# Two up projections with seven block products in place of eight in 19 of 22 tile pairs

## The chip, the core and the metric

One core of one Trainium2 chip runs the whole program. The time is the device time in microseconds. The kernel before took 1276.48 us, the median of three runs (1274.92 to 1276.8).

## The reference, cut to what matters

The model has two layers over 528 tokens (16 meta tokens and 512), width 1024, float32. Layer 0 mixes by a state-space model, layer 1 by differential attention; each is followed by this channel mixer, with D_FF = 2816:

```python
def conv_ffn(h, w_up, conv_w, conv_b, w_down):
    L = h.shape[1]
    up = h @ w_up                                   # (528, 1024) @ (1024, 5632)
    up_p = jnp.pad(up, ((0, 0), (CONV_WIDTH - 1, 0), (0, 0)))
    c = conv_b + sum(conv_w[j] * up_p[:, j:j + L] for j in range(CONV_WIDTH))
    gate, val = jnp.split(c, 2, axis=-1)
    return (jax.nn.silu(gate) * val) @ w_down       # (528, 2816) @ (2816, 1024)
```

In front of it h is normalized by rms_norm: each token by one over the root of its mean square plus 1e-6, and each channel by a gain.

## The kernel before

Everything is kept with channels on the 128 partitions and tokens along the free dimension. Float32 accuracy is had by splitting: each operand is a high part, rounded to the format that TensorE multiplies (ACT does it, `split_hi`, L297), and a low part, the rest (POOL, `split_lo`, L301). A product is three matmuls: high by high, high by low, low by high.

A unit is a weight tile of 1024 x 128, loaded by one DMA of 512 KB into one of two slots of `raw`. Its split parts go into `wH` and `wL`, four slots each. `unit_products` (L314) multiplies it by the eight tiles of the activation, for two halves of the tokens (264 columns each in layer 0, 258 in layer 1): 48 matmuls into two PSUM banks. An up projection is 22 pairs of units, a gate tile and a value tile, so 96 matmuls a pair; two pairs share the eight banks in turn.

Rounded activations are `hgH` and `hgL`, with the gain in them but not the root, which is per token and is multiplied in when DVE drains the banks into `u` (L1796, L1797). For the root, POOL sums squares into `acc` while the mixer's last projection is written (L2027, L2028), four matmuls with ones add them up (`stat_products`, L854), ACT takes the root (L1391) and DVE the reciprocal `rstd` (L1787). In the first pair the statistics stand behind 108 matmuls of the projection: both units of pair 0, and two of the eight tiles of the next unit.

Per pair DVE does, all in SBUF: two drains, the last conv tap with the bias for gate and value (TENSOR_SCALAR, L1801), two more taps of each (L1807), the product of silu and value (L1814) and the low part of the result (L1816). ACT does two weight roundings, the silu (L1402) and the rounding of the result into `actH` (L1404). POOL does two weight low parts. The order on each engine is the order of the code, in loops of two pairs; semaphores such as `up_free` (banks drained), `w_lo` (low part there), `w_used` (slot free) join the engines.

The down projection follows. In layer 0 it is 8 groups of 22 tiles by 6 matmuls of 264 columns. In layer 1 (`down_by_token`, L937) the activation is the stationary side: per tile 24 matmuls of 512 columns into all eight banks, which first take the residual by transposes (L927).

## Time and profile before

| | us |
|---|---|
| median of the runs | 1276.48 |
| span of the profiled execution | 1273.0 |
| TensorE busy (matmul) | 1243.4 |
| DVE busy | 751.6 |
| POOL busy | 607.4 |
| ACT busy | 570.7 |

The runs list no time of the profiled execution by itself. The median of the runs is 3.5 us above its span; that difference is taken for what lies around the span. Busy times of different engines overlap. A group of instructions is told by its line; L297, L301 and L314 are helpers called from several stages.

### The profile page before, as it was taken

To read this page: it belongs to the slowest core of one execution; us is meant where nothing else is said; L and a number is where in the kernel's file an instruction comes from. 1 tells how busy PE (TensorE), PEld (TensorE's weight loads), DVE (VectorE), ACT (ScalarE), POOL (GpSimd) and SP (SyncE) were. 2 spreads that over 40 slices of the span, in tenths; PEclk is the share of its full clock that TensorE was granted. 3 is DMA by queue.
4 is the path that set the end of the run, shared out by engine and by line. 5 is a ranking of instruction groups with operands and counts; after the bars stand their busy time and mean duration, and the time that the engine had idled before them with its cause. 6 is when DMAs were issued, how large, how long until landed. Compare 5 with 4: busy or idle time off the path is not lost.

```text
span 1273.0 us, 26292 instructions
## 1 busy us (share of the span) xinstructions
PE 1243.4 (98%) x10335; PEld 1185.3 (93%) x10335; DVE 751.6 (59%) x1028; ACT 570.7 (45%) x957; POOL 607.4 (48%) x361
## 2 busy tenths in 40 slices
PE   5899999999999999999999999999999999999998
PEld 5888999999999999999998988989999999998886
DVE  8997122688888884111455555553688888882002
ACT  7996543343343432222656656633243333432113
POOL 5433566444444345656654544419544344444431
PEclk9999999999999999999999999999999999999999
DMA  8333332223322333333222112113323333233231
GB/s 174 67 72 82 102 100 84 75 75 99 99 82 87 95 95 91 93 91 112 70 69 65 50 51 68 34 50 100 97 71 97 99 96 86 82 99 99 99 99 66
DMA packets 179498, 108.88 MB, mean 86 GB/s; under 512 B 7100, under 2 KB 173789, under 8 KB 179165
## 3 DMA queue, kind: packets, MB, share of 16 engines
q1 hardware_dynamic: 178997, 107.31, 30.0%
q8 instruction: 51, 0.84, 0.3%
q10 hardware_dynamic: 432, 0.59, 0.1%
q14 instruction: 18, 0.15, 0.0%
HBM read 101.59 MB, written 2.10 MB: 81 GB/s over the span
## 4 chain that ended last, share of the span: by engine, by line
PE 86%; issue 6%; POOL 4%; DVE 2%; ACT 1%; DMA 0%; SPq 0%; POOLq 0%; DVEq 0%; ACTq 0%
PE ps L314 49%; PE ps L987 10%; PE ps L937 10%; PE ps L818 7%; PE ps L1024 2%; PE ps L1094 2%; PE ps L772 1%; POOL acc L2028 1%; PE ps L764 1%; PE ps L1070 1%; POOL sqt L2027 1%; PE ps L1028 0%; PE ps L744 0%; DVE ps L1727 0%; PE ps L711 0%
## 5 line engine op out<-in xcount | busy, mean ns | idle before, releaser
L301 POOL TENSOR_TENSOR wL<-raw,wH 128x1024 fp32r<-128x1024 f32 x182 | 446.9, 2467 | 548.8 <-ACT wH L297 523.0
L314 PE MATMUL ps<-hgH,wH 128*128 128x264 f32 (+1 forms) x1408 | 285.3, 284 | 0.0
L314 PE MATMUL ps<-hgH,wL 128*128 128x264 f32 (+1 forms) x1408 | 285.3, 284 | 0.0
L314 PE MATMUL ps<-hgL,wH 128*128 128x264 f32 (+1 forms) x1408 | 285.0, 284 | 0.0
L297 ACT ACTIVATE wH<-raw 128x1024 fp32r<-128x1024 f32 x182 | 186.4, 1048 | 216.4 <-PE ps L314 79.0
L314 PEld LDWEIGHTS ps<-hgH,wH 128*128 128x128 f32 x1408 | 218.9, 189 | 0.1
L314 PEld LDWEIGHTS ps<-hgL,wH 128*128 128x128 f32 x1408 | 218.4, 189 | 0.0
L314 PEld LDWEIGHTS ps<-hgH,wL 128*128 128x128 f32 x1408 | 217.8, 189 | 0.0
L1402 ACT ACTIVATE cg<-cg 128x528 f32<-128x528 f32 (+1 forms) x44 | 28.2, 640 | 266.7 <-DVE cg L1807 266.7
L1807 DVE SCALAR_TENSOR_TENSOR cg<-u,PV,cg 128x528 f32<-128x528 f32 (+1 forms) x88 | 104.9, 1192 | 13.0 <-DVE cv L1801 6.7
L1801 DVE TENSOR_SCALAR cv<-u,PV 128x528 f32<-128x528 f32 (+1 forms) x44 | 111.3, 2530 | 0.0
L987 PE MATMUL ps<-hgH,wH 128*128 128x264 f32 x384 | 83.2, 298 | 0.0
L987 PE MATMUL ps<-hgH,wL 128*128 128x264 f32 x384 | 78.2, 285 | 0.0
L987 PE MATMUL ps<-hgL,wH 128*128 128x264 f32 x384 | 77.9, 284 | 0.0
L314 PE MATMUL ps<-actH,wL 128*128 128x264 f32 x352 | 71.2, 283 | 0.0
L314 PE MATMUL ps<-actH,wH 128*128 128x264 f32 x352 | 71.2, 283 | 0.0
L314 PE MATMUL ps<-actL,wH 128*128 128x264 f32 x352 | 71.2, 283 | 0.0
L1807 DVE SCALAR_TENSOR_TENSOR cv<-u,PV,cv 128x528 f32<-128x528 f32 (+1 forms) x88 | 66.2, 752 | 0.0
L1829 DVE TENSOR_TENSOR ytok<-ps,fgain 128x512 f32<-128x512 f32 x4 | 2.8, 692 | 103.2 <-ACT ysq L1421 103.2
L1465 ACT ACTIVATE Pb<-ps,tiny 128x144 f32<-128x144 f32 (+4 forms) x66 | 34.8, 532 | 63.2 <-DVE tiny L1855 63.1
L987 PEld LDWEIGHTS ps<-hgH,wH 128*128 128x128 f32 x384 | 59.3, 189 | 3.9 <-issue 3.8
L1763 DVE SCALAR_TENSOR_TENSOR hgL<-hT,PV,hgH (+1 forms) x24 | 34.9, 1455 | 43.2 <-ACT hgH L1373 43.2
(301 smaller groups left out, 2384.8 us busy)
## 6 DMA issues: line engine op xcount, KB each, us to landing
raw<-ffn_w_up SPq DMA_DIRECT2D x88, 512.0 KB, 3.8
raw<-ffn_w_down SPq DMA_DIRECT2D x38, 512.0 KB, 3.6
raw<-attn_w_qkv SPq DMA_DIRECT2D x24, 512.0 KB, 3.7
raw<-s_w_glu SPq DMA_DIRECT2D x16, 512.0 KB, 4.0
TT<-KD SPq DMA_DIRECT2D x64, 64.0 KB, 2.4
raw<-attn_w_o SPq DMA_DIRECT2D x8, 512.0 KB, 4.1
raw<-ffn_w_down SPq DMA_DIRECT2D x8, 384.0 KB, 3.4
xb<-x SPq DMA_DIRECT2D x8, 256.0 KB
```

The lines of the kernel that those rows point to most:

```text
L297: nc.scalar.activation(wH[:, slot, 0:nk], raw[:, slot % 2, 0:nk], ACT.Copy).then_inc(w_hi, 1)
L301: nc.gpsimd.tensor_tensor(wL[:, slot, 0:nk], raw[:, slot % 2, 0:nk], wH[:, slot, 0:nk].bitcast(F32), ALU.subtract).then_inc(w_lo, 1)
L314: mm = nc.tensor.matmul(ps[:, bank + b, 0:tw], w[:, slot, k0 + k, :], x[:, kt, t0:t0 + tw], start=first and k == 0 and s0, stop=last and k ...
L818: mm = nc.tensor.matmul(ps[:, bank + b, 0:tw], w[:, n % 4, k, :], x[:, k, t0:t0 + tw], start=k == 0 and s0, stop=k == 7 and s1)
L937: mm = nc.tensor.matmul(ps[:, 2 * t + c, :], x[:, kt, tok], w[:, n % 4, 4 * c:4 * c + 4], start=False, stop=last and w is ws[-1] and x is ...
L987: mm = nc.tensor.matmul(ps[:, unit_bank(n) + b, 0:tw], w[:, n % 4, k, :], x[:, k, t0:t0 + tw], start=k == 0 and s0, stop=k == 7 and s1)
L1024: return nc.tensor.matmul(ps_row[:, base[c] + a:base[c] + b], q[half[c], q0:nk], k[half[c], a:b], start=True, stop=stop)
L1402: nc.scalar.activation(cg[:, t0:], cg[:, t0:], ACT.Silu).then_inc(silu_set[l], 1)
L1465: ins = nc.scalar.activation(Pb[:, c, 0:nk], score_row(i, c), ACT.Exp, bias=mn[:, c:c + 1], scale=-1.0, accum_out=esum[:, c:c + 1])
L1763: V.scalar_tensor_tensor(hgL[:, ds(ct, 1)], hT[:, ds(ct, 1)], PV[:, ds(gain, 1)], hgH[:, ds(ct, 1)].bitcast(F32), ALU.mult, ALU.subtract). ...
L1801: ins = V.tensor_scalar(c[k][:, t0:], u[:, k, 2 + t0:2 + L], col(i, CONV_W + (3 * l + 2) * 2 * FT + k * FT + q), col(i, CONV_B + l * 2 * F ...
L1807: ins = V.scalar_tensor_tensor(c[k][:, t0:], u[:, k, t0 + j:L + j], col(i, CONV_W + (3 * l + j) * 2 * FT + k * FT + q), c[k][:, t0:], ALU. ...
```

## The change

The first three pairs of each layer stay as they are ("plain"). For each of the other 19 ("fast"), numbered s = 0 to 18, the pair is a 2 x 2 block product: the weights in two halves of the inner dimension (four tiles each) by gate and value, the activation in the same two halves by two halves of the tokens. Eight block products become seven of the Winograd form of Strassen's method, P1 to P7, each 4 tiles x 3 = 12 matmuls of one token half's width into one bank.

- Weight side: AA is the gate tile itself (both halves), A22 the value tile's second half, S1, S2, S3 and S4 are sums and differences of halves. DVE forms the four sums, S1 in PSUM bank 3 and the others in `Wsum`. ACT rounds all of them; POOL takes the low parts of AA, S2 with S3, S4 and A22, DVE that of S1.
- Activation side: seven factors (four quarters and T1 to T4), once per layer, from the normalized activation: `normed` makes the quarters with the gain and `rstd`, `factors` the four differences; ACT rounds seven; POOL takes the low parts of four, DVE of three. They lie where `actH` and `actL` were.
- Result side: P1, P6, P5 and P3 accumulate into one bank of the pair, P7 and P4 into the next, P2 into bank 2. ACT copies the bank after P1, P6 and P5 (`snap`), and as the last quarter (`top_right`); DVE adds three quarters into `u` or `u2`.
- The order on TensorE is P1(s), P2(s), P3(s-1), P6(s), P7(s), P4(s-1), P5(s).
- The conv of a fast pair runs in banks 6 and 7: ACT writes the last tap with the bias there, DVE adds the two others in place, gate first, then value. The last tap of plain pairs moves from DVE to ACT too.
- `act32` holds the product of silu and value; its 22 high and low parts are made after the last step's products free the factors' place.
- In the first pair the statistics stand behind 66 matmuls.
- Loops are written out. In layer 1 the token tiles use other banks, and the load of the final gain is issued on SP's queue.

TensorE, the start and the fast pairs:

```diff
+PLAIN = 3
+FAST = FT - PLAIN
...
+                    for c, k0, nk in ((0, 0, CT - 1), (1, 0, CT // 2), (1, CT // 2, CT // 2 - 1), (0, CT - 1, 1), (1, CT - 1, 1)):
+                        if l == 0 and c and k0 == 0:
+                            pe.wait_ge(glu_sig, CT)
+                        if k0 == CT // 2:
+                            stat_products(2 * l)
...
+                def product(name, s, weights, part, f, bank, first):
+                    if weights != "S1":
+                        pe.wait_ge(f_lo_pool, 4 * FAST * l + LOW_POOL[weights, s] + 1)
+                    else:
+                        pe.wait_ge(f_lo_dve, FAST * l + LOW_DVE[weights, s] + 1)
+                    at = ring(l, weights, s).start + part
+                    xH, xL = FB[:, high_at(f), :, 0:width], FB[:, low_at(f), :, 0:width]
+                    for k in range(4):
+                        for i, (w, x) in enumerate(((wHB, xH), (wHB, xL), (wLB, xH))):
+                            mm = nc.tensor.matmul(ps[:, bank, 0:width], w[:, at, k, :], x[:, k], start=first and k == 0 and i == 0,
+                                                  stop=k == 3 and i == 2, skip_group_check=True)
...
+                def free_banks(s):
+                    if s < 2:
+                        pe.wait_ge(up_free[l], PLAIN + s + FREE)
+                    else:
+                        pe.wait_ge(c12_set, FAST * l + s - 1)
+                        pe.wait_ge(c21_set, FAST * l + s - 1)
+                    return chain_bank(s), chain_bank(s) + 1
...
+                def fast(s):
+                    y, z = free_banks(s)
+                    if s == 0:
+                        pe.wait_ge(fb_hi, 7 * l + F_B11 + 1)
+                        pe.wait_ge(fb_lo_pool, 4 * l + 1)
+                    product("P1", s, "AA", 0, F_B11, y, True)
+                    if s == 0:
+                        pe.wait_ge(fb_hi, 7 * l + F_B21 + 1)
+                        pe.wait_ge(fb_lo_pool, 4 * l + 2)
+                    if s:
+                        pe.wait_ge(c11_set, FAST * l + s)
+                    product("P2", s, "AA", 1, F_B21, W_BANK, True)
+                    if s:
+                        third(s - 1)
+                    pe.wait_ge(snap1, FAST * l + s + 1)
+                    if s == 0:
+                        pe.wait_ge(fb_lo_dve, 3 * l + 1)
+                    product("P6", s, "S23", 0, F_T2, y, False)
+                    if s == 0:
+                        pe.wait_ge(fb_lo_dve, 3 * l + 2)
+                    product("P7", s, "S23", 1, F_T3, z, True)
+                    if s:
+                        fourth(s - 1)
+                    pe.wait_ge(snap2, FAST * l + s + 1)
+                    if s == 0:
+                        pe.wait_ge(fb_lo_dve, 3 * l + 3)
+                    product("P5", s, "S1", 0, F_T1, y, False)
```

TensorE, the end of the up stage and the first group of layer 0's down projection, and the start of layer 1's:

```diff
+                    else:
+                        down_part(g, 0, 0, 6)
+                        third(FAST - 1)
+                        fourth(FAST - 1)
+                        down_part(g, 0, 6, 8)
+                    down_part(g, 1, 0, 8)
+                    down_part(g, 2, 0, 6)
...
+                ready(0)
+                products(0, 2, range(2))
+                pe.wait_ge(c11_set, FAST + FAST)
                 residual(3)
+                products(0, 3, range(2))
+                last_products()
+                ready(1)
+                for t in (2, 3):
+                    products(1, t, range(2))
+                pe.wait_ge(c12_set, FAST + FAST)
+                pe.wait_ge(c21_set, FAST + FAST)
+                residual(0)
+                pe.wait_ge(act_set, FT + FT)
+                residual(1)
                 for kt in range(FT - 4):
-                    ready(kt)
```

ACT, the order of the start and of a step:

```diff
+                direct_top(0)
+                plain_taps(0)
+                sums_23(0)
+                factor_high(F_B11, 4)
+                factor_high(F_B21, 8)
+                factor_high(F_T2, 11)
+                factor_high(F_T3, 10)
+                factor_high(F_T1, 9)
+                factor_high(F_B22, 8)
+                factor_high(F_T4, 12)
+                plain_taps(1)
+                for s in range(FAST):
+                    more = s + 1 < FAST
+                    sum_1(s)
+                    if s >= 2:
+                        silu(s - 2)
+                    direct_last(s)
+                    if s >= 2:
+                        val_in(s - 2)
+                    first_snap(s)
+                    if s == 0:
+                        plain_silu(0)
+                    if more:
+                        direct_top(s + 1)
+                    else:
+                        tile_high(0)
+                    if s:
+                        top_right(s - 1)
+                    if not more:
+                        tile_high(1)
+                        down_high(0, "P2")
+                    second_snap(s)
+                    sum_4(s)
+                    if s < 2:
+                        plain_silu(s + 1)
+                    if s:
+                        gate_in(s - 1)
+                    else:
+                        plain_taps(2)
+                    if more:
+                        sums_23(s + 1)
+                    else:
+                        tile_high(2)
+                        down_high(1, "P7")
+                        tile_high(3)
+                    third_snap(s)
+                silu(FAST - 2)
+                for kt in range(4, 6):
+                    tile_high(kt)
+                val_in(FAST - 2)
+                for kt in range(6, 10):
+                    tile_high(kt)
+                top_right(FAST - 1)
+                gate_in(FAST - 1)
+                for kt in range(10, 12):
+                    tile_high(kt)
+                silu(FAST - 1)
+                down_high(2, "P3")
+                val_in(FAST - 1)
+                for kt in range(12, 16):
+                    tile_high(kt)
```

DVE, the order of the start, of a step and of the end, with three of the operations:

```diff
+                def normed(ct):
+                    h = span(hT[:, ct], spans)
+                    gain = GAIN_FFN + 8 * l + ct
+                    second = FBf[:, 0, ct, 0:width] if ct < 4 else FBf[:, low_at(F_B22), ct - 4, 0:width]
+                    first = FBf[:, low_at(F_B11 if ct < 4 else F_B21), ct % 4, 0:width]
+                    scales = span(rstd, spans)
+                    V.scalar_tensor_tensor(first, h[:, 0], PV[:, gain:gain + 1], scales[:, 0], ALU.mult, ALU.mult)
+                    V.scalar_tensor_tensor(second, h[:, 1], PV[:, gain:gain + 1], scales[:, 1], ALU.mult,
+                                           ALU.mult).then_inc(fb_set, 1)
...
+                def bottom_left(s):
+                    dve.wait_ge(f_used, len(PROD) * l + PROD["P4", s] + 1)
+                    V.tensor_tensor(quarter(PLAIN + s, 1, 0, spans), snap[:, 1 + s % 2, 0:width],
+                                    ps[:, chain_bank(s) + 1, 0:width], ALU.add).then_inc(c21_set, 1)
...
+                def bank_tap(s, c, j):
+                    o = conv_bank(l)
+                    return V.scalar_tensor_tensor(o, span(u_pair(PLAIN + s)[:, c, j:L + j], CONV_SPANS[l]), weight(PLAIN + s, c, j), o,
+                                                  ALU.mult, ALU.add)
...
+                drain(0)
+                first_sums()
+                for ct in range(CT):
+                    normed(ct)
+                factors()
+                drain(1)
+                factor_low(F_T2)
+                factor_low(F_T3)
+                factor_low(F_T1)
+                n = plain_taps(0, 1)
+                sum_4(0)
+                after(n)
+                n = plain_taps(0, 0)
+                weight_low("S1", 0)
+                after(n)
+                multiply(0)
+                drain(2)
+                for s in range(FAST):
+                    more = s + 1 < FAST
+                    if s:
+                        bottom_right(s - 1)
+                    if s:
+                        weight_low("S1", s)
+                    if more:
+                        sum_1(s + 1)
+                    if s < 2:
+                        n = plain_taps(s + 1, 1)
+                        after(n)
+                        last = plain_taps(s + 1, 0)
+                    else:
+                        last = val_tap_0(s - 2, val_tap_1(s - 2))
+                    if more:
+                        sum_2(s + 1)
+                    else:
+                        tile_low(0)
+                    if s < 2:
+                        after(last)
+                        if s == 0:
+                            top_left(0)
+                        else:
+                            multiply(2)
+                    else:
+                        bank_multiply(s - 2, last)
+                    if more:
+                        sum_3(s + 1)
+                        sum_4(s + 1)
+                    else:
+                        tile_low(1)
+                    if s:
+                        n = gate_tap_1(s - 1)
+                        bottom_left(s - 1)
+                        gate_tap_0(s - 1, n)
+                    if not more:
+                        tile_low(2)
+                    if s:
+                        top_left(s)
+                    else:
+                        multiply(1)
+                bottom_right(FAST - 1)
+                tile_low(3)
+                tile_low(4)
+                n = val_tap_1(FAST - 2)
+                tile_low(5)
+                n = val_tap_0(FAST - 2, n)
+                tile_low(6)
+                bank_multiply(FAST - 2, n)
+                for kt in range(7, 10):
+                    tile_low(kt)
+                n = gate_tap_1(FAST - 1)
+                bottom_left(FAST - 1)
+                gate_tap_0(FAST - 1, n)
+                for kt in range(10, 12):
+                    tile_low(kt)
+                n = val_tap_1(FAST - 1)
+                tile_low(12)
+                n = val_tap_0(FAST - 1, n)
+                tile_low(13)
+                bank_multiply(FAST - 1, n)
+                for kt in range(14, FT):
+                    tile_low(kt)
```

POOL:

```diff
+                weight_low("AA", 0)
+                weight_low("S23", 0)
+                factor_low(F_B11, 9)
+                factor_low(F_B21, 12)
+                factor_low(F_B22, 11)
+                weight_low("A22", 0)
+                weight_low("AA", 1)
+                weight_low("S4", 0)
+                factor_low(F_T4, 12)
+                weight_low("S23", 1)
+                weight_low("A22", 1)
+                for s in range(2, FAST):
+                    weight_low("AA", s)
+                    weight_low("S4", s - 1)
+                    weight_low("S23", s)
+                    weight_low("A22", s)
+                weight_low("S4", FAST - 1)
+                for j in range(4):
+                    split_lo(pool, nd + j, (nd + j) % 4, 8 if l else (8, 8, 6, 8)[j])
```

## Rows read from the trace of the kernel before

**Rows 1.** The page: engines, granted clock and the chain by engine.

```profile
PE 1243.4 (98%) x10335; PEld 1185.3 (93%) x10335; DVE 751.6 (59%) x1028; ACT 570.7 (45%) x957; POOL 607.4 (48%) x361
...
PEclk9999999999999999999999999999999999999999
...
PE 86%; issue 6%; POOL 4%; DVE 2%; ACT 1%; DMA 0%; SPq 0%; POOLq 0%; DVEq 0%; ACTq 0%
```

**Rows 2.** Window of layer 0's up stage: length, then busy time (instructions) of each engine.

```profile
232.00:485.00 253.00, 253.00 (x2069) 252.90 (x2068) 218.50 (x217) 99.06 (x109) 111.88 (x45) 1.00 0.30 89
```

**Rows 3.** The chain that ended last, in order: start, length, what.

```profile
218.63 13.17 PE ps L314 x108
...
232.69 373.09 PE ps L314 x3060
...
900.63 240.77 PE ps L314 x2004
```

**Rows 4.** Timeline of DVE and POOL: start, length, engine, line, operation, [idle before].

```profile
401.74 2.67 DVE L1807 SCALAR_TENSOR_TENSOR cg<-u,PV,cg 128x528 f32<-128x528 f32 x1 [0.15 <-DVE cv L1801]
...
681.03 2.38 POOL L301 TENSOR_TENSOR wL<-raw,wH 128x1024 fp32r<-128x1024 f32 x1 [3.51 <-ACT wH L297]
...
682.36 1.21 DVE L1866 SCALAR_TENSOR_TENSOR Ab<-Pb,tiny 128x144 f32<-128x144 f32 x1
...
857.20 2.35 DVE L1763 SCALAR_TENSOR_TENSOR hgL<-hT,PV,hgH 128x528 fp32r<-128x528 f32 x1 [1.01 <-ACT hgH L1373]
...
858.93 1.54 POOL L2027 TENSOR_TENSOR sqt<-hT 128x528 f32 x1
...
248.48 1.42 DVE L1801 TENSOR_SCALAR cg<-u,PV 128x528 f32<-128x528 f32 x1 [0.19 <-DVE u L1797]
...
249.82 2.63 DVE L1801 TENSOR_SCALAR cv<-u,PV 128x528 f32<-128x528 f32 x1
```

**Rows 5.** Groups by line and shape: busy, mean ns | idle before.

```profile
L297 ACT ACTIVATE wH<-raw 128x1024 fp32r<-128x1024 f32 x176 | 181.5, 1055 | 192.7 <-PE ps L937 73.2 <-PE ps L314 55.2 <-PE ps L818 23.9
...
L1807 DVE SCALAR_TENSOR_TENSOR cv<-u,PV,cv 128x528 f32<-128x528 f32 x44 | 33.5, 761 | 0.0
...
L1796 DVE TENSOR_TENSOR u<-ps,rstd 128x528 f32<-128x528 f32 x22 | 15.4, 702 | 0.2 <-PE ps L314 0.2
...
L1663 DVE TENSOR_TENSOR E<-E,tmpE 128x1024 f32<-128x1024 f32 x8 | 9.7, 1218 | 0.2
...
L551 POOL TENSOR_TENSOR F2b<-P,Bsw 128x512 f32<-128x512 f32 x8 | 9.2, 1174 | 4.3 <-PE ps L744 4.3
...
L1946 DVE TENSOR_TENSOR hT<-hT,ps 128x258 f32<-128x258 f32 x16 | 6.0, 411 | 3.1 <-PE ps L1136 3.1
```

**Rows 6.** Timeline of POOL and DVE at the start of layer 0's up stage.

```profile
224.10 1.77 POOL L2028 TENSOR_TENSOR acc<-acc,sqt 128x528 f32<-128x528 f32 x1
...
233.46 3.45 DVE L1787 RECIPROCAL rstd<-sqt 128x528 f32<-128x528 f32 x1 [8.76 <-ACT sqt L1391]
...
241.54 0.77 DVE L1807 SCALAR_TENSOR_TENSOR cg<-u,PV,cg 128x528 f32<-128x528 f32 x1 [0.15 <-DVE cv L1801]
...
242.22 0.76 DVE L1807 SCALAR_TENSOR_TENSOR cv<-u,PV,cv 128x528 f32<-128x528 f32 x1
```

**Rows 7.** Timeline of TensorE and DVE at the start of layer 1's up stage.

```profile
885.51 0.40 PE L314 MATMUL ps<-hgH,wH 128*128 128x258 f32 x2
...
899.47 1.16 PE L854 MATMUL ps<-acc,ones 128*128 128x264 f32 x4 [0.83 <-POOL acc L2028]
...
901.40 3.45 DVE L1787 RECIPROCAL rstd<-sqt 128x528 f32<-128x528 f32 x1 [8.12 <-ACT sqt L1391]
```

**Rows 8.** TensorE after an idle stretch: timeline row, then window with PEclk.

```profile
37.04 0.47 PE L709 MATMUL ps<-cst,F1b 128*128 128x128 f32 x1 [2.82 <-POOL F2b L551]
...
38.00:40.00 2.00, 2.00 (x11) 2.00 (x11) 1.93 (x4) 1.98 (x8) 2.00 (x3) 0.50 0.61 105
```

More of the change, by code:

```diff
@@ new lines, in ffn, with down_by_token @@
+                for g in range(CT):
+                    if g:
+                        pe.wait_ge(h_new[1], g - 1 + FREE)
+                        down_part(g, 0, 0, 8)
+                    else:
[5 more added lines that the diff above has]
+                    down_part(g, 2, 0, 6)
+            def down_by_token(last_products):
@@ new lines, in silu, with tile_high @@
+                def silu(s):
+                    act.wait_ge(conv_gate, FT * l + PLAIN + s + 1)
+                    nc.scalar.activation(span(conv_pair(PLAIN + s)[0], CONV_SPANS[l]), conv_bank(l), ACT.Silu).then_inc(silu_set, 1)
+                def tile_high(kt):
+                    act.wait_ge(act_set, FT * l + kt + 1)
+                    for before, t in (("P1", 0), ("P2", 4), ("P6", 8), ("P7", 12), ("P5", 16), ("P3", 20)):
+                        if kt == t:
+                            act.wait_ge(f_used, len(PROD) * l + PROD[before, FAST - 1] + 1)
+                    nc.scalar.activation(act32H[:, kt, t0:], act32[:, act_tile(kt), t0:], ACT.Copy).then_inc(act_hi, 1)
@@ L1406, in ffn @@
+                down_high(3, "P4")
+                for kt in range(16, FT):
+                    tile_high(kt)
                 if l == 0:
@@ L1783, in ffn, with step, drain @@
                 nu, nd = (U_UP0, U_DN0) if l == 0 else (U_UP1, U_DN1)
+                width = spans[0][1]
+                weight = lambda p, c, j: PV[:, CONV_W + (3 * l + j) * 2 * FT + c * FT + p:][:, 0:1]
+                steps = [0]
+                def step(ins):
+                    ins.then_inc(conv_step, 1)
+                    steps[0] += 1
+                    return steps[0]
+                def drain(p):
+                    dve.wait_ge(w_used, nu + 2 * p + 2)
+                    bank = 4 * (1 - p % 2)
+                    for c in range(2):
+                        ins = V.tensor_tensor(span(u_pair(p)[:, c, 2:2 + L], spans), pspan(bank // 2 + c, spans),
+                                              span(rstd, spans), ALU.mult)
+                    ins.then_inc(up_free[l], 1)
```

575 lines of the change are left out of this document (440 added, 135 removed).

## The prediction

> **What bounds the kernel now.** I read the page first. TensorE is busy 98% of a 1273.0 us span at the full granted clock, DVE 59%, ACT 45%, POOL 48%; the chain that ended last runs 86% over TensorE [rows 1]. So only TensorE time counts, unless another engine makes it wait. A window over layer 0's up stage says the same: TensorE idles nowhere in 253 us, and DVE, busy 218.5 us, is the next engine [rows 2]. The chain in order of time gives the pace: 3060 matmuls of 264 columns in 373.09 us, 0.1219 us each, and 2004 of 258 columns in 240.77 us, 0.1201 us each [rows 3].
>
> The last view to read is how DVE and POOL meet. A POOL subtraction with two SBUF inputs ran from 681.03 to 683.41; a DVE operation of 144 elements with two SBUF inputs, started at 682.36, took 1.21 us and ended 0.16 us behind POOL. At 401.74 such an operation took 2.67 us [rows 4] where its like takes 0.77 [rows 6]. The other way round, POOL's square, started at 858.93 under a DVE operation that ended at 859.55, took 1.54 us, so 0.92 from that end [rows 4]. The 22 drains out of PSUM, with one SBUF input, are not held: 0.702 us in the mean [rows 5]. So of the two engines one runs at a time wherever DVE reads two SBUF operands, and whoever came first finishes. The next 1024-wide subtraction of POOL gets in between two DVE operations (248.48: 1.42 us, 249.82: 2.63 us) [rows 4]. Before, this costs DVE some 3 us per pair and nobody else anything.
>
> **The change part by part.**
>
> *Matmuls.* A pair (gate and value tile) had 2 units of 48 matmuls, 96. A fast pair has 7 products of 12, 84. Nineteen pairs in each layer drop 12: 19 x 12 x 0.1219 = 27.8 us and 19 x 12 x 0.1201 = 27.4 us, **-55.2 us**. One weight load per matmul, as before. The products write one bank twelve times in a row, where two banks alternated; no row here shows 264-wide work of that kind, so I give it 0, bounds -2 and +10 (0.003 us on each of 3192). The extra waits between products: at unit borders inside the two long pieces TensorE already passes two satisfied waits without a gap [rows 3], so 0.
>
> *A step's load.* A fast pair lasts 84 x 0.1219 = 10.24 us. POOL takes low parts of 1024, 1024, 512 and 512 elements: 2 x 2.40 (2.38 in [rows 4]) + 2 x 1.24 (1.17 for 512 elsewhere [rows 5]) = 7.3 us. ACT rounds 3584 elements at 1.0 us per 1024 [rows 5], 3.7 us with the starts, and copies or taps 2640 more, some 3.6: 7.3 us. DVE does four weight sums, one low part, four conv taps and a multiply in PSUM and three quarter sums: 5 x 0.63 + 4 x 0.69 + 0.63 + 3 x 0.38 = 7.7 us by start-to-start times [rows 5], 0.9 for six waits on its own results (0.15 each [rows 6]), and behind POOL up to 1.2 and 0.9 us before sum_3 and sum_4: about 10.3. The two-input ones (sum_1, sum_3, sum_4) and POOL need 9.3 us of each other's exclusion. So the steady step is TensorE's by a hair: bottom_left must be done in the 1.46 us between P4 and the next P1, and the two sums stand ahead of it. I take +0.08 us a step, **+3 us**; bounds 0 and +19 (0.5 a step). The table loads of ACT (1.28 us, two per two pairs) go; ACT wasn't late, worth 0.
>
> *The start of the fast pairs.* This is where I differ from the plain count. Products need normalized factors, so everything hangs on the reciprocal. Layer 0: TensorE starts at 218.63 [rows 3]; the statistics now come behind 66 matmuls instead of 108, at 226.7, and acc is ready at 225.87; so the reciprocal ends near 232.2 instead of 236.91 [rows 6]. The three plain pairs end at 218.63 + 288 x 0.1219 + 0.9 = 254.6, and P1 of the third fast pair, twelve products on, could start at 272.2, 40 us after the reciprocal. Until it can, bottom_left(0) must be done, which frees its banks, and up to there DVE has: first_sums 3, plain taps 12, multiplies 3, S1's low part 1, weight sums 7 (two-input ones, 26 x 0.66 = 17.2 us), normed 16 x 0.40 = 6.4, factors and factor lows 7 x 1.17 = 8.2. That is 31.8 us with two SBUF inputs, and some 8 us more of drains and PSUM work. POOL has in that time seven subtractions of 1024 (units 4 and 5, AA and S23 of pairs 0 and 1, AA of 2), four factor lows of 1056 and four parts of 512: 16.8 + 9.9 + 5.0 = 31.7 us. Both engines need the other's absence: 63.5 us in turn, not 40. The bottom: DVE alone, 31.8 + 8 + 3 for waits = 43, so +3 us a layer; the top: no overlap with DVE's 8 us either, +32. I laid the queues out in order with these durations and the one-at-a-time rule, and P1(2) comes 64 us after the reciprocal, at 296. TensorE waits first for drain(1), queued behind the factors (3.6 us), then for snap1, snap2, c11 of pair 0 and c21 of pair 0 (2.4, 4.5, 6.2, 5.1) and for small things. **+24 us** in layer 0, and the same ledger in layer 1, where the plain pairs end at 927.3 and the reciprocal still at 904.85 [rows 7]: 944.6 becomes 968.8, **+24 us**.
>
> *The statistics moved forward.* In layer 1 TensorE already waits 0.83 us for acc, until 899.47 [rows 7]. After 66 instead of 108 matmuls from 885.51 it is there at 893.4 and waits 6.0 us, and nothing is won, since the reciprocal starts with acc: **+5 us** (bounds +4 and +6). In layer 0 no wait.
>
> *The tail.* The high and low parts of all 22 activation tiles, formerly one per pair, come at the end: 22 x 0.63 = 14 us on DVE and 22 x 0.56 = 12 on ACT, with the conv of three pairs between them. Down in layer 0 takes a tile each 6 x 0.1219 = 0.73 us. From P4(18) to tile_low(12) stand c21, two gate taps, silu, a weight split, val_in and a val tap: 6.3 us against 4.4 of matmuls; tile 21 is ready near +12.4 against 11; ahead of that the first tiles and the first down weights are 3 us late. Layer 0 **+8 us** (2 to 12). In layer 1 residual(1) needs act_set of the last tile, which comes 8.5 us behind P4, and 3.7 us of work is there: **+6 us** (3 to 8).
>
> *Clock.* TensorE idled 2.82 us before 37.04, and from 38 to 40 us the granted clock was 0.50 (1.2 GHz) [rows 8]. The waits above are of that size. Most of the slow work falls before another wait: **+5 us** (0 to 9).
>
> Pages weighed against this: the Trainium skill, VectorE: DVE Perf Modes, The DRAIN you can't avoid, has the next VectorE operation wait until the pipe of the one before is empty. Here a tap of 0.77 us is followed by the next 0.68 us after its start [rows 6], so they overlap by 0.09. By the page a step of DVE would be some 1 us longer and the steady step 11.2 us, 36 us more in all; the measurement decides and I leave it out.
>
> Sum: -55.2 + 3 + 24 + 24 + 5 + 8 + 6 + 5 = **+19.8 us**. Own time: the profiled span is 1273.0 us and the median of the runs 1276.48, so 3.5 us lie around the span, which I keep: 1273.0 + 3.5 + 19.8 = **1296 us**.
>
> **Rivals.**
> 1. *The exclusion hardly bites at the start* (POOL and DVE interleave better than in turn): then P1(2) comes near 272 + 1 and 945 + 1, no long waits, no slow clock: -55.2 + 2 + 5 + 4 + 4 = -40, about 1236; with half of the start's waits, 1260. For it: only single collisions are in the trace, never two full queues. Against it: each of these collisions shows the whole wait. The Trainium skill, SBUF — State Buffer, Who interferes with whom, has the second to issue fully blocked for the whole instruction whenever DVE reads two SBUF tensors and GpSimd reads SBUF; by it the time is the forecast's. Chance 0.24, this is the faster side.
> 2. *DVE becomes the bound in every step*: if sum_3 and sum_4 both meet a full POOL operation, the step is 10.75 us, 0.5 x 38 = +19 on top, 1315 us. For: 10.3 against 10.24. Chance 0.18.
> 3. *Slower by less*: the start costs 12 to 15 us a layer, tails as small as their bounds, 1278 to 1284. Chance 0.12, within the range.
> 4. *The matmul saving doesn't come in full*, same-bank products at 0.13 us: 2 x 19 x 84 x 0.008 = +26. Chance 0.04.
>
> **How the numbers follow.** Forecast (1285 to 1308 us) 0.42, rival 1 0.24, rival 2 0.18, rival 3 0.12, rival 4 0.04. Likeliest 1296. The range 1254 to 1316 leaves out the full rival 1 (0.13) and the far ends of 2 and 4 (0.07), 2 in 10. A change under 0.2% (2.6 us) can't be told from none; that needs a cancelling that only falls between rivals 1 and 3: 0.03. Faster 0.25, slower 0.72.
>
> **What would show it.** Right: TensorE's L314-like pace inside products unchanged at 0.122 and 0.120; gaps of 2 to 7 us each in the first 40 us of fast pairs of both layers, a granted clock of 0.5 behind them, DVE's `sum` and `factor` operations at 2 to 3 us instead of 0.7; a 6 us wait on acc at 893; a steady pair in 10.2 to 10.4 us; 64 us from the reciprocal to P1(2). Wrong: P1(2) within 45 us of the reciprocal (rival 1), or a steady pair above 10.5 us (rival 2 or 4, told apart by whether TensorE is idle in it).

## Result: 1.5% slower

Times are the medians of the runs, in microseconds; the ratio is against the kernel before on the same chip.

| kernel | time | ratio, 95% interval |
|---|---|---|
| before | 1275.87 (1274.92 to 1276.8) | 1 |
| changed | 1295.23 (1294.8 to 1295.53) | 1.0151 (1.0137 to 1.0166) |
| predicted | 1296 (1254 to 1316) | slower, chance 0.72 |

The change cost 19.4 us where 19.8 were forecast. The fast pairs do save what was counted, some 57 us; their start and their end give back 76. The experiments below win back 34 us of these: the last version runs in 1260.80 us, 34 us below the changed kernel and 15 below the one before, with the same products.

### The profile after

The page of the changed kernel: busy time of each engine, the granted clock in 40 slices, and the chain that ended last by engine.

```profile
span 1293.0 us, 25126 instructions
...
PE 1211.7 (94%) x9879; PEld 1149.6 (89%) x9879; DVE 822.6 (64%) x1215; ACT 697.8 (54%) x1283; POOL 749.1 (58%) x445
...
PEclk9899999988999998999999999999879999998999
...
PE 75%; DVE 11%; issue 7%; POOL 4%; ACT 1%; DMA 1%; SPq 0%; POOLq 0%; DVEq 0%; ACTq 0%
```

Against [rows 1]: TensorE has 31.7 us less work (456 matmuls fewer) in a span 20.0 us longer, and DVE's share of the chain went from 2% to 11%. Of the seven slices where the clock is below 9, four lie at the starts of the fast pairs (259 to 323 us and 905 to 970), one in layer 0's tail (485 to 517), one in layer 1's (1164 to 1196), and one at 32 to 65 us, ahead of all that was changed. Who holds TensorE up is in its waits (releaser, total, times, longest):

```profile
PE ps L1071 <- DVE u L2351: 10.2, 2, 5.3
...
PE ps L1071 <- issue: 8.8, 2, 4.6
...
PE ps L1071 <- ACT snap L1717: 6.6, 2, 3.8
...
PE ps L1016 <- POOL acc L2696: 6.0, 1, 6.0
...
PE ps L1180 <- DVE act L2398: 5.9, 1, 5.9
...
PE ps L1071 <- DVE u L2247: 5.7, 2, 2.9
```

L1071 is a fast product: about 33 us are waited in the products, all in the first pairs. The timeline of TensorE shows where in layer 0 (in brackets the idle time before, and its releaser):

```profile
257.96 0.51 PE L1071 MATMUL ps<-FB,wH 128*128 128x264 f32 x2 [2.82 <-DVE u L2247]
...
263.20 0.68 PE L1071 MATMUL ps<-FB,wH 128*128 128x264 f32 x2 [2.05 <-ACT snap L1711]
...
270.65 0.81 PE L1071 MATMUL ps<-FB,wH 128*128 128x264 f32 x2 [2.74 <-ACT snap L1717]
...
280.40 0.81 PE L1071 MATMUL ps<-FB,wH 128*128 128x264 f32 x2 [5.26 <-DVE u L2351]
...
295.54 0.78 PE L1071 MATMUL ps<-FB,wH 128*128 128x264 f32 x2 [4.61 <-issue]
```

These are P1(0), P6(0), P5(0), P2(1) and P1(2): 17.5 us. The two matmuls at 257.96 take 0.51 us, those at 295.54 take 0.78: the clock has fallen between them. From 295.54 on nothing waits until the last steps of the up stage. The chain has layer 0's and layer 1's long pieces:

```profile
295.54 174.23 PE ps L1071 x1416
...
977.19 171.96 PE ps L1071 x1416
```

And windows (length, then busy time and instructions of PE, PEld, DVE, ACT, POOL, granted clock, DMA share, GB/s):

```profile
297.00:302.00 5.00, 5.00 (x28) 5.00 (x28) 4.86 (x7) 2.16 (x4) 1.77 (x2) 0.61 0.38 108
302.00:312.00 10.00, 10.00 (x85) 10.00 (x84) 8.40 (x12) 6.74 (x13) 8.07 (x4) 1.00 0.20 53
...
310.00:460.00 150.00, 150.00 (x1240) 150.00 (x1239) 144.78 (x191) 102.23 (x177) 117.39 (x60) 1.00 0.38 106
```

A window also counts the matmuls that reach over its edges, so the pace is better read from one P1 to the next. A fast pair of 84 matmuls takes 10.17 us in layer 0 (0.1211 each) and 10.11 in layer 1 (0.1204); a pair of 96 took 11.75 (0.1224) and 11.53 (0.1201) before. So twelve matmuls in a row into one bank run no slower than on two alternating banks. The mean of 0.1230 over the long piece of layer 0 comes from the slow clock of its first 5 us: from P1(2) to P1(3) it is 12.68 us and not 10.17, 2.5 us more. In layer 1 it is 11.49 and not 10.11, 1.4 more.

### The profile page after: what moved, and what is told of

It is laid out like the page before. It is cut to its first block, busy times and chain, and to the rows that moved or that the text cites. A ratio compares the mean times of both kernels' runs of the same rounds, so it can differ in the third digit from the quotient of the medians.

```text
span 1293.0 us, 25126 instructions
## 1 busy us (share of the span) xinstructions
PE 1211.7 (94%) x9879; PEld 1149.6 (89%) x9879; DVE 822.6 (64%) x1215; ACT 697.8 (54%) x1283; POOL 749.1 (58%) x445
## 4 chain that ended last, share of the span: by engine, by line
PE 75%; DVE 11%; issue 7%; POOL 4%; ACT 1%; DMA 1%; SPq 0%; POOLq 0%; DVEq 0%; ACTq 0%
PE ps L1071 29%; PE ps L1248 11%; PE ps L1190 9%; PE ps L1159 9%; PE ps L980 7%; PE ps L1285 2%; DVE lows L2372 2%; PE ps L1355 1%; PE ps L934 1%; POOL acc L2696 1%; PE ps L397 1%; DVE FB L2300 1%; PE ps L926 1%; DVE FBf L2284 1%; DVE cgv L2254 1%
## 5 line engine op out<-in xcount | busy, mean ns | idle before, releaser
L384 POOL TENSOR_TENSOR wL<-raw,wH 128x1024 fp32r<-128x1024 f32 (+1 forms) x106 | 255.0, 2409 | 305.0 <-ACT wH L380 279.3
L1071 PE MATMUL ps<-FB,wH 128*128 128x264 f32 (+1 forms) x2128 | 400.3, 289 | 33.3 <-DVE u L2351 10.2
L1071 PEld LDWEIGHTS ps<-FB,wH 128*128 128x128 f32 x2128 | 341.8, 196 | 35.2 <-DVE u L2351 10.6
L1071 PE MATMUL ps<-FB,wL 128*128 128x264 f32 (+1 forms) x1064 | 308.5, 290 | 0.0
L380 ACT ACTIVATE wH<-raw 128x1024 fp32r<-128x1024 f32 (+1 forms) x106 | 110.7, 1046 | 232.2 <-PE ps L1159 93.7
L1071 PEld LDWEIGHTS ps<-FB,wL 128*128 128x128 f32 x1064 | 206.7, 194 | 0.0
L2719 POOL TENSOR_TENSOR wL<-raw,wH 128x1024 fp32r<-128x1024 f32 x76 | 153.3, 2018 | 71.4 <-ACT wH L1667 71.4
L2719 POOL TENSOR_TENSOR wL<-Wsum,wH 128x1024 fp32r<-128x1024 f32 x76 | 156.9, 2065 | 48.3 <-ACT wH L1667 48.2
L2377 DVE SCALAR_TENSOR_TENSOR ps<-u,PV,ps 128x528 f32<-128x528 f32 (+1 forms) x152 | 115.2, 758 | 15.0 <-ACT ps L1749 13.8
L1916 ACT ACTIVATE Pb<-ps,tiny 128x144 f32<-128x144 f32 (+4 forms) x66 | 34.7, 531 | 63.3 <-DVE tiny L2523 63.2
L1248 PEld LDWEIGHTS ps<-hgH,wH 128*128 128x128 f32 x384 | 59.4, 189 | 3.9 <-issue 3.8
```

The lines of the kernel that those rows point to most:

```text
L380: nc.scalar.activation(wH[:, slot, 0:nk], raw[:, slot % 2, 0:nk], ACT.Copy).then_inc(w_hi, 1)
L384: nc.gpsimd.tensor_tensor(wL[:, slot, 0:nk], raw[:, slot % 2, 0:nk], wH[:, slot, 0:nk].bitcast(F32), ALU.subtract).then_inc(w_lo, 1)
L1071: mm = nc.tensor.matmul(ps[:, bank, 0:width], w[:, at, k, :], x[:, k], start=first and k == 0 and i == 0, stop=k == 3 and i == 2, skip_gro ...
L1248: mm = nc.tensor.matmul(ps[:, unit_bank(n) + b, 0:tw], w[:, (U_QKV + n) % 4, k, :], x[:, k, t0:t0 + tw], start=k == 0 and s0, stop=k == 7 ...
L1916: ins = nc.scalar.activation(Pb[:, c, 0:nk], score_row(i, c), ACT.Exp, bias=mn[:, c:c + 1], scale=-1.0, accum_out=esum[:, c:c + 1])
L2377: return V.scalar_tensor_tensor(o, span(u_pair(PLAIN + s)[:, c, j:L + j], CONV_SPANS[l]), weight(PLAIN + s, c, j), o, ALU.mult, ALU.add)
```

## Experiments

Theory E: DVE and POOL don't work at the same time where DVE reads two operands in SBUF and POOL reads there too, so at the start their queues add up. The chief rival, D: DVE's own queue is too long, POOL beside it or not. The experiments take the changed kernel as their base (1295.23 us).

### 1 and 2. POOL computes no low parts

These two kernels leave out what the low parts add to the products and serve for the time alone. The edit, shortened:

```
- V.tensor_tensor(wLB[:, at], weight_source(name, s), wHB[:, at].bitcast(F32), ALU.subtract)
+ link(V.memset(wLB[:, at].bitcast(F32), 0.0)); V.memset(wLB[:, at].bitcast(F32), 0.0)
```

Everywhere in both up stages:

> The low parts that POOL computes in both up stages (weights of all fast pairs, four factors, units 4 and 5) are replaced by two memsets each, of the same output and about the same duration; the low parts are then zero, and POOL reads nothing. Theory E (DVE's and POOL's operations that read two SBUF operands run in turn, never together, and this sets the start of the fast pairs): the waits before the first products of fast pairs 0 to 2 go (17.5 us in layer 0, 16 us in layer 1, down to under 3 each), the tail of layer 0 loses most of its 6 us, 1236 us (1228 to 1250). Rival D (DVE's own work and the order of its queue set the start, the exclusion costs little): the waits stay at 12 us or more a layer, 1280 to 1295 us.

Only in the start (`if s < 2`, the factors, units 4 and 5):

> The same memsets, but only for the factors, units 4 and 5 and the weights of fast pairs 0 and 1; from fast pair 2 on POOL computes the low parts as before. Theory E, with the cost in the start: 1252 us (1245 to 1262), TensorE's wait before fast pair 2 ends near 276 us in place of 295.5. Rival S (the exclusion costs in the steady steps, 0.5 us a step, and not in the start): within 5 us of 1295. Rival D: 1285 to 1295 us. The difference between this kernel and the one with all memsets is what exclusion costs in the steady steps and the tails: 10 to 17 us by theory E, nearly all of it in the tail of layer 0 and not in the steps, in which TensorE never waits.

Measured 1251.50 us (ratio to before 0.9809, 0.9793 to 0.9826) and 1256.51 us (0.9850, 0.9833 to 0.9866). POOL's place in the timeline is kept within a fifth (one subtraction of 1024 took 2.4 us, the two memsets 1.96 from start to end). The kernel with memsets in the start alone, POOL and then DVE, and two of the three waits of TensorE that are left in the start of layer 0 (the third, 2.5 us before fast pair 2, stands under "issue"):

```profile
238.38 0.95 POOL L2720 MEMSET wL<- 128x1024 f32 x1 [2.69 <-ACT wH L1667]
239.39 0.96 POOL L2721 MEMSET wL<- 128x1024 f32 x1
```

```profile
234.15 0.69 DVE L2309 TENSOR_TENSOR raw<-raw 128x512 f32<-128x512 f32 x1
...
242.07 1.26 DVE L2291 TENSOR_TENSOR FBf<-FBf 128x1056 f32<-128x1056 f32 x1
...
248.10 3.58 DVE L2300 TENSOR_TENSOR FB<-FBf,FB 128x1056 fp32r<-128x1056 f32 x3
```

```profile
265.00 0.51 PE L1071 MATMUL ps<-FB,wH 128*128 128x264 f32 x2 [1.61 <-DVE u L2351]
266.98 0.51 PE L1071 MATMUL ps<-FB,wH 128*128 128x264 f32 x2 [0.25 <-ACT snap L1724]
```

The same DVE lines in the changed kernel:

```profile
235.17 2.88 DVE L2309 TENSOR_TENSOR raw<-raw 128x512 f32<-128x512 f32 x1
...
247.43 3.34 DVE L2291 TENSOR_TENSOR FBf<-FBf 128x1056 f32<-128x1056 f32 x1
...
257.82 8.23 DVE L2300 TENSOR_TENSOR FB<-FBf,FB 128x1056 fp32r<-128x1056 f32 x3
```

0.69 against 2.88, 1.26 against 3.34, 3.58 against 8.23: DVE's work is untouched, its operations no longer meet a POOL that reads. Beside the first and the last of them a memset runs, beside the one at 242.07 nothing; the next but one (L2294), with a memset beside it, takes 1.25 against 3.52. Theory E holds and D falls: 38.7 of the 44 us that all the memsets are worth come from the start. A shorter queue of POOL is no rival: a fifth of the 31.7 us that it was given is 6 us a layer at the most, and P1(2) comes 18 us sooner behind the reciprocal (45.4 against 63.2).

The remaining 5.0 us between the two kernels were expected in layer 0's tail and are not there: the waits on `lows` are 5.4 and 5.9 us. They are the wait before fast pair 2, still 2.5 us a layer in the second kernel and 0.4 in the first ("issue" 4.9 against 0.8 us in all), and 1.5 us of slow matmuls behind it in layer 1. The size for all of it was missed by 15.5 us (1236 expected, at most 1250): that figure has most of layer 0's tail gone, which would be 6 us at the most, and it isn't; what the other 9 were to be, the record doesn't say. The waits that the memsets leave as they were are those on `lows` (5.4 us), before the statistics (5.7) and before residual(1) (5.9).

### 3. The statistics of layer 1 put back

```
- if k0 == CT // 2:                                   # after 66 matmuls
+ if l == 0 and k0 == CT // 2:
      stat_products(2 * l)
...
+ unit_products(pe, nu + 2, (nu + 2) % 4, 0, hgH, hgL, spans, 0, 2, True, False, None, False)
+ if l == 1:                                          # after 108 matmuls
+     stat_products(2 * l)
```

> In layer 1 alone the sums of the statistics come after 108 matmuls again, as in the kernel before, in place of after 66. Sum of the prediction (a term of its own, 5 us): the 6.0 us wait at 907 us goes and 1290 us is left. Rival R (the start of the fast pairs hangs on the reciprocal plus 63 us, and the reciprocal on the sum on POOL, which is not moved): the wait before the statistics goes, the waits before fast pairs 0 to 2 grow by as much, 1295 us (1294 to 1296).

Measured 1289.77 us (1.0114, 1.0098 to 1.0131), 5.5 below the changed kernel. The plain term was right and my rival R fell. The timelines say why. POOL's low parts of units 4 and 5 and DVE's reciprocal in the changed kernel:

```profile
910.10 3.45 DVE L2405 RECIPROCAL rstd<-sqt 128x528 f32<-128x528 f32 x1 [9.00 <-ACT sqt L1652]
```

```profile
914.65 5.21 POOL L384 TENSOR_TENSOR wL<-raw,wH 128x1024 fp32r<-128x1024 f32 x2 [7.51 <-ACT wH L380]
```

and in this one:

```profile
908.10 3.46 DVE L2408 RECIPROCAL rstd<-sqt 128x528 f32<-128x528 f32 x1 [6.64 <-ACT sqt L1655]
```

```profile
909.09 4.77 POOL L384 TENSOR_TENSOR wL<-raw,wH 128x1024 fp32r<-128x1024 f32 x2 [2.98 <-ACT wH L380]
```

Waiting TensorE releases its weight slots later; units 4 and 5 are split later, and 5.2 us of POOL's work land behind the reciprocal, in the stretch where both queues are added up. Put back, about half of them lie beside the reciprocal (909.09 to 911.56) and 2.3 us behind it. From the reciprocal's end to P1(2) it is then 60.3 us and not 63.6. The reciprocal itself starts 2.0 us earlier: 0.85 of that is the whole stage, the rest nearly all the four statistics matmuls, which take 1.16 us at the full clock and took 2.13 behind the wait. TensorE's plain pairs get 7.4 us shorter (36.7 against 44.1), and the waits in the start take 2.9 of these back; rival R would have had them take all.

### 4. Fillers in the waits

```
+ def filler(n, bank):          # columns 264 to 511 of a bank that nobody reads then
+     for _ in range(n):
+         nc.tensor.matmul(ps[:, bank, 264:512], FB[:, high_at(F_B11), 0, 0:128], FB[:, high_at(F_B11), 0, 0:248],
+                          start=True, stop=True, skip_group_check=True)
```

> 106 matmuls of 248 columns a layer that compute nothing needed, in columns of a PSUM bank that nobody reads, put ahead of TensorE's waits in fast pairs 0 and 1 (14, 22, 36 and 34 of them), so that it is not idle there. Theory C (the idle time is what lowers the granted clock): the clock stays at 1.0 from 258 to 302 us, the waits that are left are short, the first 5 us after fast pair 2 begins run at full speed: 3.6 us less in layer 0 and 2.7 less in layer 1, 1289 us (1286 to 1292). Rival: fillers hold up the snapshots behind them and the start comes later by what they cost, 1296 to 1302 us. Third: the clock does not follow the fillers, 1295.

Measured 1291.69 us (1.0126, 1.0109 to 1.0142), 3.5 less. The output of this kernel is wrong, so it serves for the time and the clock alone. The fillers have `start` set and share a bank with P7 before P4 is added to it; that this spoils what P4 is added to is my reading, which no run tests by itself. Later kernels have both flags off, and their output is right. Windows of this kernel, to be held against the 0.61 above:

```profile
262.00:270.00 8.00, 7.21 (x60) 6.81 (x58) 8.00 (x7) 3.63 (x6) 3.60 (x2) 1.00 0.00 0
...
297.00:302.00 5.00, 5.00 (x43) 5.00 (x42) 4.86 (x10) 3.58 (x6) 4.41 (x3) 1.00 0.09 18
```

43 matmuls in place of 28 in those 5 us: the idle stretches are what lowers the clock. But P1(2) starts at 296.48, not earlier than 295.54 (76.7 and 76.5 us behind the first product of the stage): DVE's and POOL's queues set it, and the clock costs only what falls behind it. That is 2.5 and 1.4 us, not the 3.6 and 2.7 of the expectation.

### 5. The residual of token tile 1 late

```
+ products(0, 0, range(2)); products(1, 0, range(2))
+ ready(2)
+ for t in (2, 3, 0): products(2, t, range(2))
  pe.wait_ge(act_set, FT + FT)
  residual(1)
```

> In the tail of layer 1 the transposes of the residual for token tile 1, which wait for the last gated product, come behind five more groups of down products (tile 0 of weight tiles 0 and 1, tiles 2, 3 and 0 of weight tile 2). Theory: TensorE's 5.9 us wait at 1168 us is cover for 7 us of products, what is left is the wait for weight tile 2 and its low part: 1290.5 us (1289 to 1293). Rival: weight tile 2 is not split before the wait ends either, because its high part stands behind the last silu on ScalarE: 1295 us, with the wait now named by wH or wL.

Measured 1287.35 us (1.0085, 1.0067 to 1.0103), 7.9 less. The window in the changed kernel and then in this one:

```profile
1161.00:1172.00 11.00, 4.82 (x22) 4.20 (x23) 9.91 (x13) 8.39 (x14) 5.02 (x2) 0.69 0.24 73
```

```profile
1161.00:1172.00 11.00, 9.90 (x51) 7.75 (x50) 9.91 (x13) 8.40 (x14) 5.13 (x2) 1.00 0.22 61
```

5.1 us of the wait go, and the clock, 0.69 in that window, stays at 1.00, which gives another 1.4: the tail of the trace is 6.5 us shorter. The expectation (4.7 less, at the most 6.2) had no term for the clock. The medians differ by 7.9; what the last 1.4 us are, no row shows.

### 6 and 7. The start's low parts on DVE, and the order alone

```
+ def low_here(name, s):                                        # on DVE
+     dve.wait_ge(f_hi, len(HIGH) * l + HIGH[name, s] + 1)
+     V.tensor_tensor(wLB[:, at], weight_source(name, s), wHB[:, at].bitcast(F32), ALU.subtract).then_inc(f_lo_pool, 1)
...
- weight_low("AA", 0); weight_low("S23", 0); factor_low(F_B11, 9) ... weight_low("A22", 1)   # on POOL
+ pool.wait_ge(f_lo_pool, 4 * FAST * l + 7)
```

> All low parts of the start (weights of fast pairs 0 and 1, factors B11, B21, B22 and T4) move from POOL to DVE, in a new order of DVE's queue. Theory E (the two engines take turns): what is handed over takes POOL 24 us and DVE 12 us, so the sum of both queues falls, the start is shorter: by the queues laid out in order 10 us a layer, 1274 us (1268 to 1282). Rival D (no exclusion, DVE is the longer of two parallel queues): DVE gets 12 us more a layer, the start is 7 to 8 us later in each, 1310 us (1303 to 1318).

> The same new order of DVE's queue, with those low parts left on POOL as in the changed kernel: the control for the kernel before it. Theory E: the order is worth 0 to 3 us, 1293 us (1288 to 1297), and the kernel with the parts on DVE is some 20 us below it. Rival O (the gain of the other kernel is the order's): both come out within 4 us of each other.

Measured 1274.86 us (0.9992, 0.9983 to 1.0002) and 1292.08 us (1.0126, 1.0108 to 1.0145). This is the cleanest of the tests: with the same order of DVE's queue, giving DVE *more* work makes the kernel 17.2 us faster. A long queue of DVE alone (rival D) and the order alone (rival O) are both out. Chain pieces of the control and of the kernel with the parts on DVE (both begin at fast pair 3):

```profile
307.06 161.57 PE ps L1071 x1332
...
985.12 160.58 PE ps L1071 x1332
```

```profile
297.25 161.64 PE ps L1071 x1332
...
967.58 160.57 PE ps L1071 x1332
```

9.8 us earlier in layer 0, 17.5 after both starts. The pieces themselves are equally long. A factor's low part takes POOL 2.4 us and DVE 1.25; as long as one engine has to stand still, that engine's time is what counts.

### 8 to 11. Together

All of it, the low parts of units 4 and 5 on DVE too, a DVE order laid out anew, and fillers with both flags off:

> All together: low parts of the start and of units 4 and 5 on DVE in an order laid out anew, the statistics of layer 1 after 108 matmuls, the residual of token tile 1 late, and 75 filler matmuls a layer (15 before P2, 40 before P6 of fast pair 0, 20 before P2 of fast pair 1). If the parts add up: 1274.9 with the parts on DVE, less 5.5 for the statistics, less 7.9 for the residual, less 4 for the new order, less 1 to 2 for the clock: 1256 us (1252 to 1262). Rival (the statistics' gain was that of POOL's unit parts lying before the reciprocal, which is lost when DVE does them): 1262 to 1266 us.

The same without fillers:

> The same without the filler matmuls. Theory C (idle stretches of TensorE lower the granted clock for what follows): 2 to 4 us more than with them. Rival: where DVE's queue sets the start, the clock in it costs nothing, within 1 us of the kernel with fillers.

All of it with the statistics as in the changed kernel:

```
- if l == 0 and k0 == CT // 2:
+ if k0 == CT // 2:
```

> The kernel with all changes and fillers, but with the statistics of layer 1 after 66 matmuls, as in the changed kernel. It asks where the 5.5 us of the kernel with the statistics put back came from. Rival R (from POOL's low parts of units 4 and 5, which came before the reciprocal there, and which DVE now computes behind it): 1263 to 1265 us, no difference. Sum (the wait itself): 1267 to 1269 us, since TensorE waits 6 us before the statistics again.

All of it, and the weight sums of pair 0 before the reciprocal:

```
+ if j == 4:                                     # SP, ahead of unit 4's load
+     for c in range(2): sp.dma_start(pair_raw(0, c), up(PLAIN, c)).then_inc(pair_in[c], 16)
...
+ dve.wait_ge(sq_sum[2 * l], CT)
+ first_sums()
+ sum_4(0)
  dve.wait_ge(stat_sqrt[2 * l], 1)
  V.reciprocal(rstd[:, :], sqt[:, :]).then_inc(up_free[l], 1)
```

> The kernel with all changes and fillers, and also: the raw weights of fast pair 0 are loaded ahead of those of unit 4, so that DVE forms the four weight sums of pair 0 while it waits for the statistics' square root, not after the reciprocal. 2.8 us of DVE's queue behind the reciprocal go in each layer. If DVE's queue alone sets the start: 1263.3 less 2 x 1.9 (laid out in order): 1259.5 us (1257 to 1262). Rival: the loads land after the square root is there and hold up the reciprocal: 1263 to 1268 us.

| kernel | time | ratio to before, 95% interval |
|---|---|---|
| all | 1263.28 | 0.9901 (0.9885 to 0.9918) |
| without fillers | 1264.03 | 0.9908 (0.9891 to 0.9924) |
| statistics as in the change | 1265.01 | 0.9917 (0.9900 to 0.9933) |
| sums before the reciprocal | 1260.80 | 0.9882 (0.9866 to 0.9899) |

The parts don't add up to the 1256 expected. The first two and the last two ran on different chips; between the first and either of the last the intervals overlap, so 1.7 and 2.5 us are the medians' word and no more (the last two, on one chip, are 4.2 apart, beyond their intervals). The statistics' place is worth 5.5 us with POOL computing units 4 and 5, and 1.7 here, where DVE does it behind the reciprocal either way: the rival of that expectation, nearly in full.

The fillers are within the noise (0.8 us), and not because there is nothing to fill: without them TensorE waits 21.4 us in the products, and the clock is 0.84 over layer 0's start:

```profile
256.00:289.00 33.00, 23.68 (x160) 22.93 (x159) 32.57 (x44) 19.43 (x31) 6.24 (x3) 0.84 0.23 64
```

So the rival holds: where DVE's queue sets the start, the clock in it costs nothing. The early sums bring 2.5 us of the 3.8 expected, since in layer 0 the load lands late, so that part of their rival is true too:

```profile
227.52 0.69 DVE L2341 TENSOR_TENSOR Wsum<-raw 128x512 f32<-128x512 f32 x1 [3.13 <-DMA raw<-ffn_w_up]
...
230.18 3.44 DVE L2441 RECIPROCAL rstd<-sqt 128x528 f32<-128x528 f32 x1
```

The reciprocal starts 1.1 us later than the 229.08 it has with the sums behind it. The page of this kernel, and its largest waits of TensorE:

```profile
span 1258.9 us, 25428 instructions
...
PEclk9999999999999999999999999999999999999999
```

```profile
PE ps L1175 <- DVE lows L2405: 7.3, 7, 2.1
...
PE ps L1080 <- DVE u L2268: 2.9, 1, 2.9
PE ps L1080 <- DVE wL L2328: 2.7, 3, 1.0
```

These waits are short because 75 fillers a layer stand in them; they don't show what the start still costs. From the last plain matmul to P1(2) it is 31.1 us in layer 0 and 33.3 in layer 1, with 17.4 us of products in each: 29.6 us are lost, where the changed kernel lost 45.6. So of the 57 us saved the last version still gives back 42: the start in both layers is the largest part, then layer 0's tail with 11, of which 7.3 are the waits on `lows`.

## Why the prediction was right

**The bound and the mechanism.** The four collisions of [rows 4] were read as one rule, and the changed kernel is ruled by it: P1(2) came at 295.54 where laying out the queues gave 296, 63.2 us behind the end of the reciprocal against 64. The kernel without POOL's reads in the start has it at 45. That the two queues set the start, and by taking turns, is shown by experiments 1, 2, 6 and 7.

**The ledger.** Forecast, and what the times at which TensorE begins and ends each stage show:

| term | forecast, us | from the traces, us |
|---|---|---|
| matmuls | -55.2 | -57.0 |
| steady step | +3 | 0 |
| start, both layers, with the clock | +53 | +49.5 |
| statistics, layer 1 | +5 | +7.5 |
| tail, layer 0 | +8 | +11.2 |
| tail, layer 1 | +6 | +8.0 |
| other stages | 0 | +0.8 |
| sum | +19.8 | +20.0 |

They come from these times, at which the first product of a stretch starts on TensorE (or the last one ends), and from the time per pair given above:

| us from the span's start | before | changed |
|---|---|---|
| layer 0: up stage | 218.47 | 219.01 |
| plain pairs done | 254.54 | 255.14 |
| P1(2) | | 295.54 |
| down stage | 477.72 | |
| QKV | 605.62 | 612.98 |
| layer 1: up stage | 885.51 | 893.14 |
| plain pairs done | 922.10 | 937.20 |
| P1(2) | | 977.19 |
| down stage | 1141.24 | |
| last product ends | 1267.63 | 1287.69 |

**Matmuls.** Right: 19 x (11.75 - 10.17) and 19 x (11.53 - 10.11) are 30.0 and 27.0 us. The twelve in a row into one bank cost nothing.

**Steady step, +3.** It cost 0: no wait of TensorE in either long piece, and with POOL's reads gone from every step (experiment 1) a pair takes the same 10.17 us. DVE's 10.3 us were too much: it is busy 144.8 of 150 us in the window above, 9.8 us a pair, and keeps up. Rival 2, which rested on it, falls.

**Start, +24 and +24, and the clock, +5.** Best judged together: 53 forecast, 49.5 measured. In layer 0, 17.5 us of waits; from 257.96 to the end of P5(1) at 290.93 lie 12 products in 22.9 us without the waits, 5.5 more than 144 x 0.1211; with the 2.5 behind P1(2) that is 25.5. In layer 1, 15.8 + 6.8 + 1.4 = 24.0. The division was wrong: I had 21.8 us of waits in layer 0 and little clock. The slow products fill part of a wait that would be there anyway, which is why the fillers, with the clock at 1.00 throughout, bring back 3.5 us and not the 16 that slow products took.

**Statistics, +5.** The wait was right, 5.96 us (0.83 before). Behind it the slow clock takes another 2.3, which I left out: the plain pairs of layer 1 last 44.1 us against 36.6. My argument ("nothing is won, since the reciprocal starts with acc") left out that the wait also shifts POOL's work behind the reciprocal; in experiment 3 this second part is 3.3 of the 4.5 us by which P1(2) comes earlier in its stage.

**Tails, +8 and +6.** Both cost more. Layer 0: 11.2 us, of which waits are 6.5 and slow matmuls behind them 2.3; 2.4 are in no row that I can name.

```profile
490.00:494.00 4.00, 2.78 (x13) 2.81 (x13) 4.00 (x5) 2.20 (x4) 2.72 (x3) 0.50 0.37 100
```

The first piece of QKV, before and after, is 7.4 us later:

```profile
605.78 6.60 PE ps L987 x54
```

```profile
613.14 6.58 PE ps L1248 x54
```

0.5 of that is there when the up stage begins (219.17 against 218.63), so the layer costs 6.8, against +8.2 by my terms (-27.8 + 1.5 + 24 + 8 + 2.5). Layer 1: 8.0 us, 5.92 of them the wait before residual(1) and 1.4 the slow clock behind it.

**Around the span.** I kept 3.5 us, the median of the runs less the span of the profiled execution. By the same count it was 2.2 (1295.23 - 1293.0), but that mixes executions: the profiled one took 1294.8 us, 1.8 more than its own span. The span was 1293.0 against 1292.8 by the terms. That is closer than the terms deserve and in part luck: the start, the steady step and the matmuls came out 8.3 us below their terms, the statistics, the tails and the rest 8.5 above.

**The rivals.** Rival 1 (0.24) named the right quantity and mis-sized it: it has 60 us between no exclusion and the forecast, where the memsets in the start bring 38.7, to 1256.51, and those everywhere 43.7. The sum behind rival 3 doesn't come out: with 12 to 15 us a layer for the start, 1296 becomes 1272 to 1278, and less with small tails, not 1278 to 1284. Rival 4 falls with the pace above.

## To carry to other kernels

Where two engines exclude each other, add their queues up over the stretch in which both have work; the sum against the third engine's work in that stretch is the bound. The busy shares don't show it, for the time an operation is held counts as busy: between the reciprocal and P1(2) in layer 0 DVE is busy 62.5 of 63.2 us and POOL 39.7, for 31.7 us of work by its own durations. Handing work to the slower of the two is then a loss even when the other looks full: price it at the time on the engine that does it. A scheme that saves per step (some 1.5 us a pair here) must be charged with its fixed start and end, here 36.7 us in layer 0 (25.5 + 11.2) and 39.5 in layer 1 (24.0 + 7.5 + 8.0) against 30 and 27 saved; 34 of these 76 us could be moved away, 42 are still there.

## What the runs showed beyond that

- The clock matters only behind the last wait of a stretch that another engine sets: with it at 0.50 to 0.83 in the start, or held at 1.00 by fillers, P1(2) came within 1 us of the same time. Behind a wait that nobody else covers it counts in full: in layer 1's tail 1.4 us of slow matmuls come on top of 5.9 of waiting.
- The exclusion costs both sides. In the changed kernel's start three low parts of factors on DVE took 8.23 us and one on POOL 3.35; with nothing to exclude they take 3.58 on DVE and 2.45 on POOL.
- A DVE operation with one operand in PSUM isn't held up. In the changed kernel, POOL's subtraction and DVE's queue beside it:

```profile
295.16 2.38 POOL L2719 TENSOR_TENSOR wL<-Wsum,wH 128x1024 fp32r<-128x1024 f32 x1 [4.40 <-ACT wH L1667]
```

```profile
295.37 0.76 DVE L2377 SCALAR_TENSOR_TENSOR ps<-u,PV,ps 128x528 f32<-128x528 f32 x1
...
296.72 0.67 DVE L2345 TENSOR_TENSOR wL<-ps,wH 128x512 fp32r<-128x512 f32 x1
```

Both keep their 0.7 us inside POOL's 2.38. So in these rows it is the operand's place that decides. Sums kept in PSUM might be a further way out of the start's cost; that wasn't tried, since all banks are taken there.
